# A fused attention, recurrence and mixture-of-experts layer on one core: loads, waits and order of work in the output projection and in the last norm

## The reference

```
proj = x @ w_in
a = rms_norm(mla_group(...), mla_out_g)          # 8 heads of attention, 512 columns
r = hgrn2_group(...)                             # 4 heads of a gated recurrence, 512 columns
mix = concatenate([a, r]) @ w_out                # 1024 x 1024
h = layer_norm(ALPHA * x + mix, ln1_g, ln1_b)
moe = hier_moe(h, ...)                           # router, top 2 of 32 experts
out = layer_norm(ALPHA * h + moe, ln2_g, ln2_b)
```

## Time and profile before

| | |
|---|---|
| median of 3 runs | 2511.37 us |
| the profiled execution | 2508.14 us, its span 2506.3 us |
| busy: PE, DVE, ACT, POOL | 2263.5 (90%), 1611.1 (64%), 1204.0 (48%), 323.1 (13%) us |
| third stage | 1249.9 to about 1540 us |
| last norm | about 2440 to 2506.3 us |
| granted clock of PE, mean | 0.96 |

### The profile page before, as it was taken

How to read it: one execution, slowest core, us unless ns; L and a number is a source line. 1 busy time by engine, 2 the same in 40 slices (tenths; PEclk the granted TensorE clock), 3 DMA queues, 4 the chain that set the end, 5 groups by cost and what they waited for, 6 DMA issues and landing times. The chain is left out here.

```text
span 2506.3 us, 42808 instructions
## 1 busy us (share of the span) xinstructions
PE 2263.5 (90%) x13202; PEld 1847.6 (74%) x13203; DVE 1611.1 (64%) x2940; ACT 1204.0 (48%) x1974; POOL 323.1 (13%) x215
## 2 busy tenths in 40 slices
PE   7999999999999999999869996899999999999950
PEld 7999988896666666766657775787777788888840
DVE  5444445456767767777645776687886765666537
ACT  4333343226666656656532220465665555446426
POOL 0000000000000000000001110113342332322312
PEclk9999999999999999999979997899999999999975
DMA  4121112250000000000053334699989978887826
GB/s 174 72 89 67 59 59 88 92 164 28 8 5 10 12 6 11 12 9 6 20 189 115 129 134 159 208 356 310 365 314 357 336 228 290 284 257 262 271 75 248
DMA packets 157230, 368.19 MB, mean 147 GB/s; under 512 B 25792, under 2 KB 37824, under 8 KB 155200
## 3 DMA queue, kind: packets, MB, share of 16 engines
q1 hardware_dynamic: 142592, 318.88, 35.0%
q0 software_dynamic: 13104, 47.72, 7.8%
q10 hardware_dynamic: 1440, 0.37, 0.1%
HBM read 295.11 MB, written 72.35 MB: 147 GB/s over the span
## 5 line engine op out<-in xcount | busy, mean ns | idle before, releaser
L1917 PE MATMUL eH<-w_hi,at_tok 128*128 128x512 f32 x720 | 285.9, 397 | 11.8 <-DVE at_tok L2035 11.5
L1968 ACT CAST w_hi<-w_raw 128x4096 fp32r (+1 forms) x64 | 232.7, 3636 | 111.8 <-DMA w_raw<-in_w 78.4
L1977 DVE TENSOR_TENSOR w_raw<-w_raw,w_hi 128x4096 f32 (+1 forms) x64 | 282.4, 4414 | 0.0
L1918 PE MATMUL eH<-w_hi,at_tok 128*128 128x512 f32 x720 | 281.5, 391 | 0.0
L963 PE MATMUL pS<-kT,qT 128*128 128x512 f32 (+3 forms) x640 | 260.7, 534 | 4.7 <-ACT pr L1052 4.3
L1060 ACT CAST prT_hi<-pT 128x512 fp32r<-128x512 f32 (+1 forms) x288 | 162.3, 563 | 199.1 <-PE pT L973 198.7
L1147 DVE TENSOR_TENSOR prT_lo<-pT,prT_hi 128x512 fp32r<-128x512 f32 (+1 forms) x288 | 189.3, 658 | 93.6 <-ACT prT_hi L1060 93.1
L1977 DVE TENSOR_TENSOR w_raw<-w_raw,at_row 128x4096 f32 x32 | 141.6, 4424 | 115.1 <-ACT at_row L1968 114.7
L1138 DVE TENSOR_REDUCE mx<-pS 128x1 f32<-128x512 f32 (+2 forms) x320 | 191.4, 607 | 15.5 <-PE pS L963 9.0
L1922 PE MATMUL eH<-w_raw,at_tok 128*128 x720 | 180.3, 392 | 12.2 <-DVE w_raw L1977 12.2
L963 PEld LDWEIGHTS pS<-kT,qT 128*128 128x128 f32 x640 | 111.4, 190 | 106.6 <-issue 63.2
(11 more groups left out here) (363 smaller groups left out, 5274.0 us busy)
## 6 DMA issues: line engine op xcount, KB each, us to landing
w_raw<-in_w SPq DMA_DIRECT2D x96, 2048.0 KB, 14.1
xt<-in_x SPq DMA_DIRECT2D x9, 1024.0 KB, 8.1
xs<-in_x SPq DMA_DIRECT2D x8, 1024.0 KB, 5.1
scratch_h<-hp SPq DMA_DIRECT2D x16, 512.0 KB, 2.7
scratch_z<-hp SPq DMA_DIRECT2D x16, 512.0 KB, 4.0
fz<-scratch_z SPq DMA_DIRECT2D x16, 512.0 KB, 10.6
out<-fz SPq DMA_DIRECT2D x16, 512.0 KB, 2.6
scratch_xT<-xT_hi SPq DMA_DIRECT2D x7, 1024.0 KB, 3.9
```

Source lines behind the costliest of these rows:

```text
L1917: pe.matmul(H[:], xh[:, k, :], w.hi[:, k, :], start=(k == 0), stop=False)
L1918: pe.matmul(H[:], xl[:, k, :], w.hi[:, k, :], start=False, stop=False)
L1968: nc.scalar.copy(w.hi[:], w.words(o).bitcast(F32)).then_inc(w.hi_ready, 1)
L1977: v.tensor_tensor(w.words(o), w.words(o).bitcast(F32), w.hi[:].bitcast(F32), ALU.subtract).then_inc(w.lo_ready, 1)
```

## The change

Five edits in the third stage and one in the last norm; the arithmetic is the same.

1. The first four pieces of `w_out` (4 to 7) are loaded in the attention, after its last preparation, into `cqn`, which nobody reads any more (`wo_raw`). In the third stage ACT and DVE split them before anything else. The other four go to `hp` and `hT` without waiting for a place. `at_row` and `at_tok` change places with other tiles so that nothing written early lies on `cqn`.
2. PE's first pair begins with the recurrent shares of both tiles, then both turns, then both attention shares (`begin`).
3. SP issues the next pair's `rts`, then `ap`, as its step begins, before the stores of tile 0.
4. ACT's norm of the next `ap` (`norm_a`) comes after `sd` and the first cast of the next `rts`; DVE's `invert` after the statistics of tile 0.
5. The waits for constants are put where they are first used.
6. In the last norm statistics run a pair ahead of the norm; one short instruction replaces three, one reciprocal serves two tiles.

```diff
+                    if n == LAST_PREP + 1:
+                        sp.wait_ge(prep, len(PREP_NO))
+                        for k in range(4):
+                            sp.dma_start(t["wo_raw"][:, k], w_out[:, 4 + k]).then_inc(t["wo_raw_loaded"][k], 16)
                     if n % (2 * NQ) == NQ - 1 and 1 < h // 2 + 1 < HEADS // 2:
...
                 def step(m, last):
                     if not last:
+                        sp.wait_ge(rl_ready, m * 2 + 2)
+                        sp.dma_start(rts[:], rT[:, :, bass.ds((m + 1) * 2 * P, 2 * P)]).then_inc(r_loaded, 16)
                         sp.wait_ge(a_norm, m * 2 + 2)
                         sp.dma_start(ap[:], ad[m + 1]).then_inc(a_loaded, 16)
                     for i in range(2):
                         if i == 1 and not last:
-                            sp.wait_ge(rl_ready, m * 2 + 2)
-                            sp.dma_start(rts[:], rT[:, :, bass.ds((m + 1) * 2 * P, 2 * P)]).then_inc(r_loaded, 16)
                             sp.wait_ge(res, m * 4 + 4)
...
+                def begin():
+
+                    share(0, 0, 1)
+                    share(0, 1, 1)
+                    turn_a(0, 0)
+                    turn_a(0, 1)
+                    share(0, 0, 0)
+                    share(0, 1, 0)
+                    route(0, 0)
...
                         if not last:
                             split_r(m + 1, i)
+                            if i == 0:
+                                norm_a(m + 1, False)
                     turned(m * 2, 0)
-                split_r(0, 0)
-                split_r(0, 1)
-                attention(0, True)
                 for n, k in enumerate(W_ORDER):
-                    act.wait_ge(w_loaded[n % 4], n // 4 * 16 + 16)
                     if n == 4:
-                        act.wait_ge(c_loaded, 3 * 16)
+                        split_r(0, 0)
+                        split_r(0, 1)
+                        measure_a(0, True)
+                        norm_a(0, True)
+                        act.wait_ge(ga_loaded, 16)
+                    act.wait_ge(w_loaded[n], 16)
...
-                    if not last:
-                        invert(m + 1)
                     for i in range(2):
                         v.wait_ge(mixed, m * 2 + 1 + i)
...
                         v.bn_aggr(mv[:, i, :], st[:, i]).then_inc(aggr, 1)
+                        if i == 0 and not last:
+                            invert(m + 1)
                         v.wait_ge(root, m * 2 + i + 1)
...
-                    v.tensor_scalar(mean, s1[:, i:i + 1], 1.0 / DM, None, ALU.mult).then_inc(moments, 1)
-                    v.wait_ge(moments, i)
-                    v.tensor_scalar(s1[:, i:i + 1], mean, mean, None, ALU.mult).then_inc(moments, 1)
-                    v.wait_ge(moments, i + 1)
-                    v.tensor_scalar(var, s2[:, i:i + 1], 1.0 / DM, s1[:, i:i + 1], ALU.mult, ALU.subtract).then_inc(aggr, 1)
+                    v.scalar_tensor_tensor(less, mean, mean, s2[:, i:i + 1], ALU.mult, ALU.subtract).then_inc(spread, 1)
...
-                for i in range(0, NT, 2):
+                gain(0)
+                measure(4)
+                moment(3)
+                factors(2)
+                gain(1)
+                for i in range(2, NT, 2):
+                    if i + 2 < NT:
+                        moment(i + 3)
                     gain(i)
                     if i + 2 < NT:
-                        measure(i + 2)
-                        moment(i + 3)
                         factors(i + 2)
+                    if i + 4 < NT:
+                        measure(i + 4)
                     gain(i + 1)
-                    if i + 2 < NT:
-                        factors(i + 3)
```

More of the change, by code:

```diff
@@ L834 @@
 NTB = 2
+LAST_PREP = max(n for n in range(NI) for i in range(2) if prep_in(n, i))
 def phase_b(nc, t, d):
@@ L1352, in _ @@
             def _(pe):
-                def project(m, i):
[L1356 to L1373, removed]
@@ new lines, in share @@
+                def share(m, i, part):
+                    if part == 1 and (not isinstance(m, int) or m > 0):
+                        pe.wait_ge(res, m * 4 + 2 * i - 2)
+                    if i == 0 and isinstance(m, int) and m == 0:
+                        pe.wait_ge(wl_ready, 8 - 4 * part)
+                    hi, lo = (ah, al) if part == 0 else (rh, rl)
+                    pe.wait_ge(ah_ready if part == 0 else rh_ready, m * 2 + i + 1)
+                    pe.wait_ge(al_ready if part == 0 else rl_ready, m * 2 + i + 1)
+                    for half in range(2):
+                        at = slice(half * 512, (half + 1) * 512)
+                        for k in range(4):
+                            w = wh[:, 4 * part + k, at], wl[:, 4 * part + k, at]
+                            for n, (x, y) in enumerate(((hi, w[0]), (lo, w[0]), (hi, w[1]))):
+                                ins = pe.matmul(M[2 * i + half][:], x[:, i, k, :], y, start=(part == 1 and k == 0 and n == 0),
+                                                stop=(part == 0 and k == 3 and n == 2))
+                    if part == 0:
+                        ins.then_inc(mixed, 1)
@@ L1442, in turned, with measure_a @@
                     nc.scalar.copy(hT[:, i, 4:8, :], H[1][:].rearrange("p (k n) -> p k n", k=4)).then_inc(hT_act, 1)
[L1444 removed]
+                def measure_a(m, first):
                     for i in range(2):
@@ L1557, in step @@
                         v.wait_ge(h_steps, m * 4 + 2 * i + 1)
+                        if first and i == 0:
+                            v.wait_ge(g_loaded, 32)
                         v.tensor_tensor(hp[:, i], hp[:, i], g1[:], ALU.mult).then_inc(h_steps, 1)
@@ L2166, in factors @@
                 def factors(i):
-                    v.wait_ge(root, i + 1)
-                    v.reciprocal(rstd[:, i:i + 1], sd[:, i:i + 1]).then_inc(factored, 1)
-                    v.wait_ge(factored, i * 2 + 1)
-                    v.tensor_scalar(nmr[:, i:i + 1], mv[:, i, 0:1], rstd[:, i:i + 1], -1.0, ALU.mult, ALU.mult).then_inc(factored, 1)
+                    v.wait_ge(root, i + 2)
+                    v.reciprocal(rstd[:, i:i + 2], sd[:, i:i + 2]).then_inc(factored, 1)
+                    v.wait_ge(factored, i // 2 * 3 + 1)
+                    for n in range(i, i + 2):
+                        v.tensor_scalar(nmr[:, n:n + 1], mv[:, n, 0:1], rstd[:, n:n + 1], -1.0, ALU.mult, ALU.mult).then_inc(factored, 1)
                 def gain(i):
@@ L2208, in build @@
         t["x_loaded"] = ctx.enter_context(nc.semaphore("x_loaded"))
+        t["wo_raw_loaded"] = [ctx.enter_context(nc.semaphore(f"wo_raw_loaded{i}")) for i in range(4)]
         with ExitStack() as attn:
@@ L2255, in route_and_experts @@
             keep(ctx, name, [P] + shape)
-        for name in ("at_row", "at_tok"):
-            keep(ctx, name, [P, 2, NT, P], F32R)
         phase_c(nc, t, d)
```

100 lines of the change are left out of this document (58 added, 42 removed).

## The result

The changed kernel takes 2476.2 us (median of 4 runs, 2475.9 to 2479.7) against 2511.7 (4 runs, 2510.0 to 2512.4): ratio 0.9859, 95% interval 0.9848 to 0.9870. That is 35.5 us gained where 40.8 were forecast; the time is inside the range (2462 to 2484), 5.7 us above the forecast and at the upper edge of the narrower 2465 to 2476 that the forecast gave itself.

The account below looks back on a forecast made before the run. PE bounds the third stage: start -15.3, steady pairs -21.5, tail -1.6, low clock +1.2, last norm -3.6 sum to -40.8; from profiled 2508.14 that gives 2467.3, plus 3.2 is 2470.5 us. Range 2462 to 2484, narrower 2465 to 2476 (chance 0.76).

Parts of the forecast that it names:

- Start: Third stage's beginning up to the second pair's first product: early-loaded weights let PE start sooner; -15.3 us.
- the new wait: Third stage's start: PE waits 2.3 us for the norm before transposing h, which the old order did not have.
- Steady pairs: Six pairs of the third stage: PE's rts and turn waits go, pairs take 28.8 us for 32.0; -21.5 us.
- rival (a): Steady pair: DVE takes PE's place as bound, the 1.6 us turn wait stays in 6 pairs; 2480 us, chance 0.14.
- Low clock after the new wait: Third stage's start: PE's clock may drop behind the 2.3 us wait; half of 2.4 us taken, +1.2 us.
- Rival (b): Third stage's start: clock stays low longer, +2.5 to +5 us, 2473 to 2476; inside the narrower range's chance of 0.76.
- rival (c): Each pair: late ap holds DVE's first norm; landings from 14.7 us on make the change slower than before; chance 0.02.
- The last norm: From 2439.8 us to the end: a pair's period falls from 6.87 to 6.1 us; -3.6 us.
- rival (d): Last norm: fnmr and its like are held by POOL, 6 x 1.7 = +10 us, 2481; chance 0.02.
- The early load: Attention, after its 52nd output: SP's four DMAs of 2 MB cost zero, at worst 2 us.
- The experts' stage between is not touched; it starts earlier and does the same: Experts' stage, between third stage and last norm: takes the same time as before, no term in the sum.
- the offset from the profiled run to the median: Whole kernel: median of the runs lies 3.2 us above the profiled run, added to 2467.3 us.

Follow-up runs that it names:

- experiment 8: The changed kernel with the last norm put back as it was before the change; 2480.5 us.
- experiment 7: The changed kernel without its early load: the first four output-weight pieces are loaded when the third stage begins; 2485.7 us.
- experiment 2: The kernel before, with only at_row and at_tok allocated first, as in the changed kernel; 2518.0 us, ratio to before 1.0024.
- experiment 1: The changed kernel with last allocated ahead of at_row and at_tok, so their addresses again leave 224 by 256; 2471.5 us, ratio to before 0.9841.
- experiment 3: experiment 1 with ass and ars allocated behind hT, so anT_hi and anT_lo leave 224 by 256 like wo_hi and wo_lo; 2468.9 us.
- experiment 6: The changed kernel with rts issued again behind the stores of the pair's first tile, not at the head of SP's step; 2496.3 us.
- experiment 5: experiment 3 with start addresses of every large pair of stationary and streamed tile made equal by 256; 2458.6 us.
- experiment 10: experiment 5 with PE's second recurrent share ahead of the first turn of h, and DVE adding b to the last four tiles; 2449.2 us.
- experiment 9: experiment 3 with 32 bytes of padding behind last, so the experts' tiles leave 0 by 256; 2458.8 us.
- experiment 4: Separate kernel, TensorE alone: groups of 48 products of 512 columns at varied address rests; 11.02 or 11.03 us equal, mostly 11.26 to 11.35 unequal.
- experiment 11: Separate kernel: products of 256 and 512 columns, then 2 MB loads, at varied address rests; loads 5.12 us at rest 0, 5.42 at the others.

## Why the prediction was right, and where it was off

Right, by its own steps:
- Start (-15.3): -14.8 from the stage's start on. PE at +6.4 forecast, +6.47 found; the new wait 2.3 forecast (its own times, 1283.15 and 1285.8, give 2.65), 2.66 found; second pair at 1287.1 forecast, which with the stage's start 1.4 us later is 1288.5, found 1288.98.
- Steady pairs (-21.5): -22.1. 28.4 and five of 28.8 forecast, 28.25 and 28.7 found; the tail -1.7 for -1.6. DVE kept its small reserve: rival (a) is out, PE waits for anT_lo in no pair but the first.
- Low clock after the new wait (+1.2): it did not come. Counted from the stage's start, experts' first cast is 38.6 us earlier, and 37.2 or 38.4 were the forecasts with and without it. Rival (b), whose 2473 to 2476 the time would have fitted, is out by the clock alone, 1.00 in this stretch:

```profile
1285.00:1296.00 11.00, 8.34 (x46) 7.10 (x46) 7.23 (x14) 2.38 (x5) 5.42 (x2) 1.00 0.66 243
```

- ap behind other transfers: landings 5.0 to 8.8 us for 4.4 to 8.3, far from the 14.7 of rival (c).
- The last norm (-3.6): -4.1, and -4.3 by experiment 8. fnmr is not held: rival (d) is out. The odd product took 1.71, not 1.4.
- The early load at nothing: shown by experiment 7.

What failed is the step "The experts' stage between is not touched; it starts earlier and does the same". Its instructions are, its tiles' addresses are not: the hunk that allocates at_row and at_tok first made 2520 of its products (720 at each of three lines, 360 at a fourth) 6 ns dearer. The hunk stood in the diff and was passed over as bookkeeping. It has a price of 8.9 us in the trace of the changed kernel, 6.1 in the median by experiment 2, 4.7 by experiment 1. Put the addresses back and the sum comes out: experiment 1 is 2471.5, forecast 2470.5. That the time of the changed kernel still lay inside the range is luck in part: the range was wide for other reasons, and the term that failed stood at nothing.

The other term is the offset from the profiled run to the median, 3.2 us in the forecast; the changed kernel's profiled run was only 0.3 below its median, so these 2.9 us took back part of the 8.9. The profiled run of before spent 33.2 us from the attention's first product to its first output product (the attention begins at 587.4 us, not at about 500), and the same code spends 36.5 in experiments 1, 2, 3, 6, 7, 8 and in the changed kernel. The difference is TensorE's clock, before and changed:

```profile
585.00:622.00 37.00, 33.30 (x123) 17.91 (x123) 24.69 (x57) 25.69 (x57) 3.77 (x2) 1.00 0.08 22
```

```profile
585.00:622.00 37.00, 34.92 (x115) 18.17 (x116) 22.66 (x53) 23.93 (x52) 3.77 (x2) 0.91 0.08 22
```

A clock of 0.91 over 37 us is 6.8 us at the lower level, and it costs the 3.3. Experiments 5 and 10 have 1.00 there and 33.2 and 33.5 us, experiment 9 more of the lower level and 38.2. PE's wait ahead of the attention is 1.97 or 1.98 us in all of them, so the wait alone does not decide it; what does is open. Adding the median's offset was right, and a difference of the two profiles alone (32.3 us) would have understated the gain.

## What to carry to other kernels

A diff that moves a tensor changes every product and load that uses it; list the start addresses by 256 of streamed and stationary tiles and of landing buffers before and after. Keep pairs of 512-column fp32r products equal by 256, and land large loads on multiples of 256: here 2476.2 to 2458.8 us for 32 bytes of padding and three small tensors moved (experiment 9). When an undone edit gives the forecast time, look at its parts as well: the total of experiment 6 was right with a pair wrong by 1.3 us. And compare the granted clock of a stretch of identical code before reading a few microseconds between two profiles as an effect.

## What the runs showed of the hardware that was not expected

- An fp32r product of 128x128 by 128x512 has a pitch of 0.2275 us with the streamed and the stationary tile's start equal by 256 (or 16 apart), 0.229 at m - s = 64, 0.2330 at the other differences tried (experiments 4 and 11); with 256 columns equality is no gain (5.87 us a group of 48 against 5.59 to 5.87).
- 2 MB in rows of 2 KB land in 5.12 us (409 GB/s) at multiples of 256 and in 5.42 us (387 GB/s) at rests 32, 64, 128, 192 and 224 (experiment 11).
- Two fnmr instructions of 128x1 in 0.34 us lie within POOL's add, while a g product of 128x1024 (alone 1.22 us) that starts 0.3 us behind the add's start takes 3.15 us and one that starts 1.7 us into it takes 1.71; both end 1.1 us after the add.
- The same code behind the same PE wait of 1.97 or 1.98 us runs at a granted clock of 1.00 in some executions and has 6.8 us at the lower level in others: 33.2 or 36.5 us.
